# Bringing the last two expert pairs' results back to the tokens by weighted 0/1 products on TensorE, in a two-block transformer with a mixture of experts

## What is computed

```
u = rms_norm(h)                                   # 256 tokens x 1024
for each token: choose one of 4 groups, in it the 2 best of 8 experts (32 experts in all)
w1, w2 = softmax over the two chosen * group weight
y[token] = w1 * expert[e1](u[token]) + w2 * expert[e2](u[token])
           # expert: (silu(u @ gate) * (u @ up)) @ down, hidden width 256
out = rms_norm(h + y) * norm_final
```

## Time and profile before

| | us |
|---|---|
| runs, median (lowest to highest) | 1252.14 (1250.96 to 1252.32) |
| profiled execution, its own time | 1252.81 |
| its span | 1251.0 |
| TensorE busy | 1204.6 |
| TensorE weight load busy | 1025.1 |
| VectorE busy | 783.7 |
| ScalarE busy | 607.9 |
| GpSimd busy | 99.0 |

### The profile page before, as it was taken

How to read it: one execution, slowest core, us unless ns; L and a number is a source line. 1 busy time by engine, 2 the same in 40 slices (tenths; PEclk the granted TensorE clock), 3 DMA queues, 4 the chain that set the end, 5 groups by cost and what they waited for, 6 DMA issues and landing times. The chain is left out here.

```text
span 1251.0 us, 22407 instructions
## 1 busy us (share of the span) xinstructions
PE 1204.6 (96%) x9053; PEld 1025.1 (82%) x9056; DVE 783.7 (63%) x1316; ACT 607.9 (49%) x993; POOL 99.0 (8%) x102
## 2 busy tenths in 40 slices
PE   9999999999999999999999998999999999999992
PEld 7989999999899999899999998899999843333320
DVE  6876655556755555999899979869645562122113
ACT  6665544445644454667755576765545321111101
POOL 0000100000100000000000030001100004341401
PEclk9999999999999999999999999999999999999997
DMA  8653555554455655355444274355543999999993
GB/s 301 198 173 131 191 179 186 183 196 141 139 192 175 200 170 184 113 180 161 162 153 150 77 235 170 135 174 164 189 158 101 417 347 413 418 412 412 412 412 137
DMA packets 161045, 270.28 MB, mean 216 GB/s; under 512 B 17625, under 2 KB 126142, under 8 KB 156862
## 3 DMA queue, kind: packets, MB, share of 16 engines
q1 hardware_dynamic: 149872, 260.53, 59.0%
q0 software_dynamic: 10720, 8.42, 2.3%
q10 hardware_dynamic: 366, 0.12, 0.0%
HBM read 287.89 MB, written 13.63 MB: 241 GB/s over the span
## 5 line engine op out<-in xcount | busy, mean ns | idle before, releaser
L2128 DVE TENSOR_TENSOR weights_parts<-ring,weights_parts 128x1024 fp32r<-128x1024 f32 (+3 forms) x312 | 363.3, 1184 | 149.4 <-ACT weights_parts L1546 149.0
L1546 ACT ACTIVATE weights_parts<-ring 128x1024 fp32r<-128x1024 f32 (+3 forms) x312 | 308.7, 1010 | 156.5 <-PE psum L885 156.2
L883 PE MATMUL psum<-xnorm_parts,weights_parts 128*128 128x256 f32 x852 | 244.7, 287 | 4.9 <-DVE xnorm_parts L2276 2.0
L885 PE MATMUL psum<-xnorm_parts,weights_parts 128*128 128x256 f32 x852 | 238.8, 280 | 0.0
L884 PE MATMUL psum<-xnorm_parts,weights_parts 128*128 128x256 f32 x852 | 238.8, 280 | 0.0
L883 PE MATMUL psum<-expert_cols,weights_parts 128*128 128x256 f32 (+1 forms) x688 | 195.2, 284 | 3.2 <-DVE expert_cols L2146 2.0
L884 PE MATMUL psum<-expert_cols,weights_parts 128*128 128x256 f32 (+1 forms) x688 | 192.8, 280 | 0.0
L885 PE MATMUL psum<-expert_cols,weights_parts 128*128 128x256 f32 (+1 forms) x688 | 192.8, 280 | 0.0
L883 PE MATMUL psum<-hidden_parts,weights_parts 128*128 128x256 f32 x640 | 181.7, 284 | 2.4 <-DVE hidden_parts L2599 1.7
L885 PE MATMUL psum<-hidden_parts,weights_parts 128*128 128x256 f32 x640 | 180.2, 281 | 0.0
L884 PE MATMUL psum<-hidden_parts,weights_parts 128*128 128x256 f32 x640 | 180.1, 281 | 0.0
(11 more groups left out here) (452 smaller groups left out, 1724.7 us busy)
## 6 DMA issues: line engine op xcount, KB each, us to landing
ring<-in_mlp_w_up SPq DMA_DIRECT2D x32, 1024.0 KB, 5.3
ring<-in_mlp_w_down SPq DMA_DIRECT2D x32, 1024.0 KB, 4.8
ring<-in_w_in SPq DMA_DIRECT2D x30, 1024.0 KB, 5.0
ring<-in_attn_w_qkv SPq DMA_DIRECT2D x12, 1024.0 KB, 6.0
expert_raw<-in_w_exp_gate SPq DMA_DIRECT2D x22, 512.0 KB
expert_raw<-in_w_exp_up SPq DMA_DIRECT2D x22, 512.0 KB
ring<-in_w_exp_down SPq DMA_DIRECT2D x9, 1024.0 KB
expert_raw<-in_w_exp_down SPq DMA_DIRECT2D x9, 1024.0 KB
```

The source lines that it names most:

```text
L883: pe.matmul(out, lh, rh, start=start, stop=False, **more)
L885: return pe.matmul(out, ll, rh, start=False, stop=stop, **more)
L1546: ins = act.activation(high, src, ACT.Copy)
L2128: ins = dve.tensor_tensor(low, src, high.bitcast(F32), ALU.subtract)
```

## The change

The last block in the order (LAST = 19) and the one before it no longer go through the table in HBM. Blocks 0 to 17 are scattered as before, and the gather starts when those scatters have landed and the last window copies are done; table rows of the last two blocks stay zero. For the last two blocks a matrix back is built: for block q of the two it has, at (row, token), the weight w1 or w2 if that row is that token's result, else zero. way_back (VectorE, round 6) builds it with tokens on partitions, turn_back (TensorE, behind down(6) in round 7) transposes its four 128x128 tiles, copy_back (VectorE, round 8) copies them out. rows_back multiplies the tiles by the blocks' result rows and accumulates both blocks in four PSUM banks. VectorE adds the weighted gathered rows to x in place, then the products. Both halves of the last block's copy are now ScalarE's. The order at the end on TensorE and of the last weights is changed: down(18) runs, and its weights are loaded, ahead of gate_up(19).

```diff
 def ring_order():
     uses = [("gates", 0, 0), ("gates", 0, 1)]
-    for n in range(1, NB):
+    for n in range(1, LAST):
         uses += [("gates", n, 0), ("gates", n, 1), ("down", n - 1, None)]
-    return uses + [("down", NB - 1, None)]
+    return uses + [("down", LAST - 1, None), ("gates", LAST, 0), ("gates", LAST, 1), ("down", LAST, None)]
...
-        y_sum = results[:, 4 * D:6 * D].rearrange("p (b d) -> p b d", b=TB)
+        y_sum = x_nat
+        back_nat = hid_plain[:, 512:1024].rearrange("p (b q r) -> p b q r", b=TB, q=2)
+        back = hid_plain[:, 512:1024].rearrange("p (q b t) -> p q b t", q=2, b=TB)
+        sum_bank = ((0, 2), (4, 5))
...
+            def turn_back():
+                pe.wait_ge(s["back_ready"], 8)
+                for q in range(2):
+                    for tb in range(TB):
+                        mm = pe.transpose(bank(2 + TURNED_IN % 2)[:, (2 * q + tb) * P:(2 * q + tb + 1) * P],
+                                          back_nat[:, tb, q, :], ident)
+                mm.then_inc(s["back_turned"], 1)
+            def rows_back(q, half):
+                n = LAST - 1 + q
+                pe.wait_ge(s[("y_first", "y_second")[half]], n + 1)
+                for tb in range(TB):
+                    mm = pe.matmul(bank(sum_bank[half][tb]), back[:, q, tb, :], y_rows[:, n % 2, half * 512:(half + 1) * 512],
+                                   start=(q == 0), stop=(q == 1))
+                    if q == 1:
+                        mm.then_inc(s["rows_back"], 1)
-            for n in range(NB + 1):
-                if n < NB:
-                    gate_up(n, 0)
+            for n in range(LAST):
+                gate_up(n, 0)
                 if n:
+                    if n == TURNED_IN + 1:
+                        pe.wait_ge(s["back_copied"], 1)
                     turn_act(n - 1)
-                if n < NB:
-                    gate_up(n, 1)
+                gate_up(n, 1)
                 if n:
                     down(n - 1)
+                if n == TURNED_IN:
+                    turn_back()
+            turn_act(LAST - 1)
+            down(LAST - 1)
+            gate_up(LAST, 0)
+            rows_back(0, 0)
+            gate_up(LAST, 1)
+            rows_back(0, 1)
+            turn_act(LAST)
+            down(LAST)
+            rows_back(1, 0)
+            rows_back(1, 1)
```

ScalarE's end takes the halves in the other nesting (first half of both token blocks, then the second), each square behind VectorE's add:

```diff
+            copy_y(LAST)
+            act.wait_ge(s["y_full"], 2 * LAST + 2)
+            act.activation(y_rows[:, LAST % 2, 512:], bank(4 + 2 * (LAST % 2) + 1), ACT.Copy).then_inc(s["y_second"], 1)
+            for half in range(2):
+                part = slice(half * 512, (half + 1) * 512)
+                for tb in range(TB):
+                    act.wait_ge(s["rows_added"], 2 * half + tb + 1)
...
```

VectorE:

```diff
+            def way_back():
+                for choice, w in enumerate(("w1", "w2")):
+                    ins = dve.tensor_tensor(placed[:, choice], chosen[:, choice], spread(rt(w), NE), ALU.mult)
+                link(ins)
+                link(dve.tensor_tensor(placed[:, 0], placed[:, 0], placed[:, 1], ALU.add))
+                link(dve.tensor_tensor(placed[:, 1], rt("late"), same(window_at[:, 0:NE], TB), ALU.subtract))
+                for q in range(2):
+                    for e in range(2):
+                        slot = 2 * ORDER[LAST - 1 + q] + e
+                        for tb in range(TB):
+                            dve.tensor_scalar(back_nat[:, tb, q, ROWS * e:ROWS * (e + 1)], count_row,
+                                              placed[:, 1, tb, slot:slot + 1], placed[:, 0, tb, slot:slot + 1],
+                                              ALU.is_equal, ALU.mult).then_inc(s["back_ready"], 1)
+            def copy_back():
+                dve.wait_ge(s["back_turned"], 1)
+                dve.tensor_copy(hid_plain[:, 512:1024], bank(2 + TURNED_IN % 2)).then_inc(s["back_copied"], 1)
...
+            for tb in range(TB):
+                for choice, w in enumerate(("w1", "w2")):
+                    dve.wait_ge(s[f"back_in{tb}{choice}"], 16)
+                    link(dve.scalar_tensor_tensor(y_sum[:, tb, :], y_back[:, choice, tb, :], rt(w)[:, tb, :], y_sum[:, tb, :],
+                                                  ALU.mult, ALU.add))
+            for half in range(2):
+                part = slice(half * 512, (half + 1) * 512)
+                for tb in range(TB):
+                    if half and tb:
+                        dve.wait_ge(s["final_sums"], TB)
+                        dve.tensor_scalar(half_mean, sums[:, 0:TB], 1.0 / D, EPS, ALU.mult, ALU.add).then_inc(s["half_mean"], 1)
+                    dve.wait_ge(s["rows_back"], 2 * half + tb + 1)
+                    dve.tensor_tensor(y_sum[:, tb, part], bank(sum_bank[half][tb]), y_sum[:, tb, part],
+                                      ALU.add).then_inc(s["rows_added"], 1)
```

GpSimd:

```diff
-            for n in range(NB):
+            for n in range(LAST - 1):
                 pool.wait_ge(s["y_first"], n + 1)
...
             for i in range(2):
-                pool.wait_ge(y_stored[i], 16 * ((NB + 1 - i) // 2))
+                pool.wait_ge(y_stored[i], 16 * ((LAST - i) // 2))
+            pool.wait_ge(s["window_first"], NB)
+            pool.wait_ge(s["window_second"], NB)
             gather()
```

More of the change, by code:

```diff
@@ L85 @@
 RING = 17
+LAST = NB - 1
+TURNED_IN = 7
 EXTRA_AFTER = (5, 8, 10, 13)
@@ L543, in build_two_blocks @@
             "const_in", "const_rest", "first_rows_in", "more_rows_in", "x_in", "mem_in", "band_in", "pos_in", "par_in", "router_in", "zeros_set",
-            "gain_in", "final_in", "back_in00", "back_in01", "back_in10", "back_in11", "gates_half", "gates_full", "y_full", "scaled_x", "x_squared", "half_mean", "root_done",
+            "gain_in", "final_in", "back_in00", "back_in01", "back_in10", "back_in11", "back_ready", "back_turned", "back_copied", "rows_back", "rows_added", "gates_half", "gates_full", "y_full", "scaled_x", "x_squared", "half_mean", "root_done",
             "rstd_ready", "masks_ready", "cleared", "nat_high", "nat_low", "sort_ready", "sorted_full", "sorted_even",
@@ L2085, in _ @@
                     window_first(n + 1)
-                if n >= 2:
+                if 2 <= n <= LAST:
                     copy_y(n - 2)
-            copy_y(NB - 1)
+                if n == LAST:
+                    copy_y(n - 1)
             act.activation(roots[:, 0:1], eps_col[:, 0:1], ACT.Sqrt)
[L2091 to L2094, removed]
+            copy_y(LAST)
[5 more added lines that the diff above has]
+                    act.wait_ge(s["rows_added"], 2 * half + tb + 1)
                     act.activation(y_back[:, 0, tb, part], y_sum[:, tb, part], ACT.Square,
                                    accum_out=sums[:, 2 * half + tb:2 * half + tb + 1]).then_inc(s["final_sums"], 1)
[L2097 to L2100, removed]
+                    if half == 1:
+                        act.wait_ge(s["half_mean"], 2)
+                        act.wait_ge(s["final_sums"], 3 + tb)
+                        act.activation(roots[:, 2 + tb:3 + tb], sums[:, 2 + tb:3 + tb], ACT.Sqrt, bias=half_mean[:, tb:tb + 1],
+                                       scale=1.0 / D).then_inc(s["final_root"], 1)
         @block.vector
@@ L2976, in _ @@
                     window_second(n + 1)
-                if n >= 2:
+                if 2 <= n <= LAST:
                     copy_y(n - 2)
+                if n == TURNED_IN + 1:
+                    copy_back()
                 copy_acts(n - 1)
+                if n == LAST:
+                    copy_y(n - 1)
                 for part in ((), (1, 2), (3, 4), (5,))[n] if n < 4 else ():
                     more_blocks(part)
-                if n in (4, 5):
-                    (places, mixing_weights)[n - 4]()
@@ L2984, in _ @@
-            copy_y(NB - 1)
-            dve.wait_ge(s["final_in"], 16)
[L2988 to L3002, removed]
-                                             y_sum[:, tb, part], ALU.mult, ALU.add).then_inc(s["y_scaled"], 1)
-                half_mean_of(tb)
+                if n in (4, 5, 6):
+                    (places, mixing_weights, way_back)[n - 4]()
@@ L3005, in _ @@
+            dve.wait_ge(s["final_in"], 16)
+            dve.wait_ge(s["rows_added"], 4)
             for tb in range(TB):
```

2 lines of the change are left out of this document (added).

## The result

| | before | changed |
|---|---|---|
| runs, median (lowest to highest), us | 1252.14 (1250.96 to 1254.8) | 1245.15 (1243.98 to 1246.25) |
| profiled execution, its span | 1252.81, 1251.0 | 1245.27, 1243.2 |
| first gate product begins | 1008.04 | 1009.96 |
| from there to the end of the span | 242.96 | 233.24 |
| TensorE busy | 1204.6 | 1214.5 |

Faster by 0.7%: ratio 0.9929, 95% interval 0.9912 to 0.9946, against 1243.3 forecast (range 1240.8 to 1247.3). Two later sets of runs, each beside the kernel before, gave 0.9919 both times (intervals 0.9906 to 0.9933 and 0.9902 to 0.9936).

A forecast was written before the change was run, and what follows sets the result against it. Bound by TensorE and DMA level up to 1215 us, then 22.4 us with TensorE idle; last add at 1236.4 plus 5.8 gives 1242.2 against 1251.0, so 1252.14 - 8.8 = 1243.3 us, range 1240.8 to 1247.3.

The forecast's parts named there:

- The likeliest case: At the end, TensorE's side and the gathers' side meet at about 1242 us in the span; 1240.8 to 1244.9, chance 0.70.
- What goes: Gather waits for block 17's scatter in place of block 19's: two scatters less, trigger 18.7 us earlier.
- turn_back: Four transposes on full TensorE, behind down(6) in round 7: paid, 0.88 us, TensorE 0.9 later up to the end.
- copy_back at nothing: VectorE's copy of the turned tiles, round 8: hidden behind gate_up(8, 0), cost nothing; uncovered 0.7 us.
- signs of being wrong: Named beforehand: a TensorE gap in rounds 7 or 8, or half_mean or the squares setting the pace between the adds.
- way_back at nothing: Building the matrix on VectorE in round 6, where it has room: cost nothing; uncovered 2.7 us.
- TensorE's end: Last blocks' products on TensorE: down(19) ends at 1231.35, 2.8 us later than before; last rows_back ends at 1234.95.
- rows_back: Added products of 128x512 on TensorE: 1.8 us for two, bounds 0.9 and 3.6.
- The gathers: Four gathers issued 1220.9 to 1224.85, fourth landing at 1232.0, last wide VectorE operation ending at 1233.3.
- Rival B: Gathers collide with the last weights, delaying down(19): 2.2 to 4.0 us more, end at 1245.5 to 1247.3; chance 0.22.
- C: Gathers crawl beside the weights, so the kernel is slower: 1254.3 us if they move at 100 GB/s; chance 0.04.
- D: The gather still waits for something at the end of block 19, so the time stays at 1252 us; chance 0.04.

The follow-up runs named there:

- e13: Changed kernel with the matrix turned and copied in rounds 15 and 16 in place of 7 and 8; 1246.13 us, ratio 0.9919 to the kernel before.
- e4: The changed kernel run again without an edit; 1245.17 us, ratio 0.9919 to the kernel before.
- e12: The changed kernel run a third time without an edit; 1244.12 us, ratio 0.9919 to the kernel before.
- e8: Changed kernel without block 17's scatter, so the gathers are issued amid the weight stream; 1248.32 us, ratio 0.9946 to the kernel before.
- e2: Kernel before with only the new order of the last products, weights and copies; 1254.71 us, ratio 0.9997 to the kernel before.
- e3: Changed kernel with the last products and weights in the old order; 1244.67 us, ratio 0.9918 to the kernel before.
- e5: Changed kernel whose gather also waits for the last gate product of block 19; 1249.74 us, ratio 0.9960 to the kernel before.
- e10: Changed kernel with copy_back moved ahead of copy_y(6) in VectorE's round 8; 1246.21 us, ratio 0.9928 to the kernel before.

## Why the prediction was right

The likeliest case came, in its direction, its range and, but for one step (the gathers, below), its mechanism; the price was 1.85 us off. Counted from the first gate product (1008.04 before), step by step, with the first profile of the changed kernel:

| | predicted | changed kernel |
|---|---|---|
| scatter of block 17 issued | 204.36 | 204.36 |
| first gather issued | 212.86 | 213.25 |
| gate_up(19, 0) ends | 211.21 | 210.99 |
| two products of rows_back | 1.8 | 1.92 |
| down(19) begins | 219.71 | 219.14 |
| last product ends | 226.91 | 226.43 |
| last wide operation ends | 225.26 | 224.49 |
| last add ends | 228.36 | 227.37 |
| end | 234.16 | 233.24 |

- **What goes.** Right: the scatters of blocks 18 and 19 and the wait of the gather are gone, 17.8 us at the trigger, and both sides came in behind it as forecast. Of the 17.8, 9.7 reached the end: the first gather moved by 12.4 (225.67 to 213.25), as block 17's scatter took 8.89 to the first gather where block 19's took 3.53; the first landing took 1.7 more than before (5.99 from its issue to its use, against 4.29 in the earlier trace rows); and from the first wide operation to the end it is now 14.0 in place of 13.0.
- **turn_back.** 0.88 taken, 0.74 measured (e13). **copy_back at nothing** was wrong in the place where the change put it: 0.2 to 1.0 us (87.13 to 87.96, less 86.20 and 0.74), since a wait of VectorE of about 5 us, which costs nothing in the kernel before, ends just before TensorE needs the copy. The 0.7 that I gave as its uncovered price is the time of the copy itself; that it lies in the measured range is luck. TensorE's gap in round 8 is one of the signs of being wrong that I had named, and it came: 0.96 in e4, 0.32 in e12. **way_back at nothing** held: up to block 6, TensorE's times in the changed kernel are those of before to 0.01 us.
- **TensorE's end** came 0.5 early. The largest part is the turning of block 19 with its copy: 0.90 from the end of the matrix products to the start of down(19) (1228.20 to 1229.10), where I added 0.45 and 0.8. That 0.8 was read where the copy stood behind copy_y(18) on VectorE (1223.80 to 1224.49); in the changed kernel nothing stands ahead of it there. The rest is that groups of 16 instructions follow one another sooner than their records say: 3.48 from the start of down(18) to that of gate_up(19, 0), where I added 3.65.
- **rows_back.** 1.92 and 1.82 for two products (1220.88 to 1222.80, and 1226.38 to 1228.20), next to the 1.8 that went by streamed columns, and far from both bounds, 0.9 and 3.6.
- **The gathers** were the step with the wrong mechanism. I had the fourth landing set the wide operations, at 1232.0. In the changed kernel none of the last three waited: four ran in one piece of 5.25 behind the first. What starts that piece is the first landing or copy_acts(19), which stands ahead of it on VectorE and for which the sum had no term: the copy ended 0.15 before the landing in the first profile, and in e4 and e12 no wait for a gather shows at all. The adds ran three in a row, with 0.28 for half_mean where I took 0.4. Together 1.0 us to the good at the last add. A second of those signs came in part: half_mean and the squares did set the start of the fourth add.
- **Rival B** did not come, and e8 shows that it is real: with the gathers 11 us earlier it costs 4 us. The 2.2 to 4.0 was priced for a later and lighter collision than that one, which no run shows. C (a crawl) is out: 329 GB/s in 1225 to 1230. D is out: without block 17's scatter the gathers are issued 11 us earlier (e8).
- **The term that was off** is none of the change's: the median stood 1.95 above the profile's span where I took 1.14 from the kernel before (0.8), and the stage began 1.9 later in that profile; the stage itself was 0.9 better. 1.9 + 0.8 - 0.9 is the error of 1.85 but for rounding, so the price of the stage was 0.9 off and the rest is what lies ahead of it and around it. On the first chip the two kernels' medians were 7.0 apart, in the two later sets 10.2 and 11.4; from the first gate product on it is 9.0 to 9.7 in the three profiles. Taken off 1252.14, the later two would give 1241.9 and 1240.8, the low end of the range: that the median came out above the forecast and not below it is luck of the first set.
- **The order** of the last blocks, which the prediction carried along without a price of its own, is worth nothing measurable (e2, e3). I had not foreseen that: weights are late in either order (1.76 in e2, 1.08 in e3), and a hand-over that one order covers the other opens.

## What to carry to other kernels

The result's trip through HBM set the end here by its last trigger, so it paid to keep the last few pieces of work off that trip, even for extra products: some 8 us of products and transposes moved the trigger 17.8 us forward and gained 9.0 to 9.7. Here it helped to start the transfer where the stream of weights had just run out; the same gathers 11 us earlier, amid the stream, gave 4 us of the gain back. And measure such a change from the start of its stage, since what lies ahead of it (3.5 us between profiles here) moves by more than its fine points (0.7).

## What the runs showed of the hardware

- A float32 product of 128x128 by 128x512 at full width takes 0.91 to 0.96 us here, in two instructions (1.82 and 1.92 for two, from start to start of what follows). Four half-width instructions of the same columns, run two by two, take nearly the same: 0.87 to 0.90 (3.48 to 3.58 for 16).
- With work in both DMA queues, each had half of the time of the 16 engines (50.4% and 48.5% in 3 us of e8), though one carried 172 packets and the other 121 in that time.
- An indirect gather of 512 KB took 4.36 us from issue to use with no weights beside it (e5), 5.96 in the changed kernel with some 0.2 MB of weights left. The Trainium skill's fit (DMA: Bandwidth & Descriptors, Anatomy of one DMA) makes 3.2 of it, an estimate; the trace does not agree.
- VectorE stood still for 4.3 to 5.6 us in each round in which GpSimd issued eight indirect DMAs, even for a copy from PSUM whose own semaphore had long been set (e10: turn_back had ended 3 us before it ran). Its cause is open.
